# Differential attention on one core: the difference of the two maps moved from VectorE to GpSimd, the reciprocals moved ahead of the maxima

## The chip, the core and the metric

The kernel runs on one core of a Trainium2 chip. The metric is the device time of one execution in microseconds. Five engines run side by side, each with its own queue in order, and meet at semaphores: TensorE (PE; its weight loads are listed as PEld), VectorE (DVE), ScalarE (ACT), GpSimd (POOL) and SyncE (SP, which issues the DMAs).

## What is computed

The reference is one layer of a backbone, run for 128 context tokens and 1024 latent tokens: a SwiGLU feed-forward, then attention beside a recurrent unit, then a second feed-forward. The change touches the attention alone:

```python
# 4 heads; each has two maps (m = 0, 1) over 64 dimensions, values of 128
s = jnp.einsum('bqhmd,bkhmd->bhmqk', qi, k) * scale
p = jax.nn.softmax(s, axis=-1)
pd = p[:, :, 0] - lam * p[:, :, 1]
o = jnp.einsum('bhqk,bkhv->bqhv', pd, v)
...
o = _rmsnorm(o, subln_g) * (1.0 - lam_init)
mix = jnp.concatenate([o, rg], axis=-1) @ w_out
```

Context tokens attend to 128 keys, latent tokens to 1152 (1024 of their own and 128 cached).

## The kernel before

The attention stage is a pipeline over 36 tiles u = 0 to 35: 4 heads of 9 tiles with 128 queries each. The first tile of a head has the context queries and one group of 128 keys (a short tile), the other eight have nine groups (long tiles). Maps are not divided by their sums. With sums S0 and S1 of the exponentials, a tile keeps e0 + c * e1 with c = -lam * S0 / S1, and the attended values are multiplied by 1 / S0 at the end.

What a long tile needs, and on which engine:

- TensorE, `scores(u)` (L1011): two maps of 128 x 1152 into PSUM, in six pieces that alternate between the maps, `PIECES = ((0, 0, 512), (0, 512, 1024), (1, 0, 512), (0, 1024, UNIT), (1, 512, 1024), (1, 1024, UNIT))`. The first piece of map m waits for the exponential that read that map's banks before.
- VectorE, `maxima(u, m)` (L2221): the negated maximum of each row.
- ScalarE, `exps(u, m)` (L1540): the exponential into one of three buffers `pr`, with the row sums in `sums`; `e_done` counts them.
- VectorE, `difference(u)` (L2227, L2228, L2230): the reciprocals of the two sums, the coefficient `coef`, and one fused instruction that multiplies the second map by it and adds the first; `pd_ready` counts tiles.
- TensorE, `group(u, g)` (L1026): transposes of 3 x 3 blocks through one PSUM bank (bank 6). The first waits for `pd_ready`, each further one for the copy of the group before (`t_done`). ScalarE copies groups 0 and 2 (L1533), VectorE group 1 (`p_copy`, L2243).
- TensorE, `values(u, part)` (L1040), VectorE, `output(u)` (L2236): the values, and their scaling by 1 / S0. ScalarE squares them for the norm (L1548).

The order is written out by hand. In iteration u, TensorE does the scores of u, the transposes of u - 2 and the values of u - 3, mixed. VectorE does the maxima of u, the copy of u - 2, the difference of u - 1 and the output of u - 3. ScalarE does the copy of group 0 of u - 2, both exponentials of u, the copy of group 2, and the squares of u - 4. At iterations 35 and 36 VectorE also splits weights for the next stage (L1643), and from iteration 36 ScalarE and VectorE split the inputs of the output projection (L1564, L1567, L2250, L2253).

GpSimd does two things. It rotates the last head's keys (L672 to L675), which TensorE needs only at tile 27. And when VectorE has inverted the norms of the first three heads (L2274, iteration 32), it multiplies their outputs by them in 27 instructions of 128 x 128 (L682), chunk after chunk of 384 tokens. TensorE's `outputs(c, hd)` wait for these, at iteration 36 for chunk 0 and later for chunks 1 and 2.

Of the kernel before, what the change touches and what calls it, by code (L numbers as in the profile page):

```python
# [19 lines left out]
ALU = mybir.AluOpType  # L20
# [9 lines left out]
NC = T // CH  # L30
# [5 lines left out]
NH = 4  # L36
# [21 lines left out]
TILES = NH * QT  # L58
# [50 lines left out]
def build(nc, a, out):  # L109
    ctx = ExitStack()  # L110
    with ctx:
        def sem(name):
            return ctx.enter_context(nc.semaphore(name))

        def sb(name, shape, dt=F32, stack=ctx):
            return stack.enter_context(nc.sbuf_tensor("sb_" + name, shape, dt))
# [58 lines left out]
        with ExitStack() as s:  # L175
            cosT = sb("cosT", [P, LAT], F32, s)
            sinT = sb("sinT", [P, LAT], F32, s)
            swp = sb("swp", [P, LAT], F32, s)
# [5 lines left out]
            sums = sb("sums", [P, 3, 2], F32, s)  # L184
            rec = sb("rec", [P, 6, 2], F32, s)
            coef = sb("coef", [P, 3], F32, s)
            ss = sb("ss", [P, NH, 9], F32, s)
            lams = sb("lams", [P, 4], F32, s)
            nlam = sb("nlam", [P, 1], F32, s)
# [84 lines left out]
        lam_e = sem("lam_e")  # L274
        swapped = sem("swapped")
        roped = sem("roped")
        last_rope = sem("last_rope")
        s_ready = sem("s_ready")
        mx_ready = sem("mx_ready")
        e_done = sem("e_done")  # L280
        pd_ready = sem("pd_ready")
        t_ready = sem("t_ready")
        t_done = sem("t_done")
# [4 lines left out]
        o_rec = sem("o_rec")  # L288
        o_nrm_pool = sem("o_nrm_pool")
# [5 lines left out]
        w_ready = sem("w_ready")  # L295
        w_x = sem("w_x")
        y_done = sem("y_done")
        passed = [sem(f'passed{e}') for e in range(2)]
        y_out = sem("y_out")

        ssf = ss[:].rearrange("p h t -> p (h t)")
# [7 lines left out]
        def probs(u, m):  # L309
            return pr[:, u % 3, m, 0:KEY_TILES[u % QT] * P]  # L310
# [9 lines left out]
        def attended(hd, t):  # L320

            return o_first[:, t * P:(t + 1) * P] if hd == 0 else v[:, t, (hd - 1) * P:hd * P]

        def hv(h, c, k):

            return h[:, (c * KT + k) * CH:(c * KT + k + 1) * CH]
# [114 lines left out]
        def alone(eng):  # L441


            eng.sem_inc(passed[eng is nc.vector], 1)


        @blk.sync
# [218 lines left out]
        @blk.gpsimd  # L666
        def _(pool):

            xt = x[:, KT - 1, CTX:T]
            pool.wait_ge(acst, N_ACST)  # L670
            pool.wait_ge(swapped, 1)
            pool.tensor_tensor(xt, xt, cosT[:], ALU.mult).then_inc(last_rope, 1)  # L672
            pool.tensor_tensor(swp[:], swp[:], sinT[:], ALU.mult).then_inc(last_rope, 1)
            pool.wait_ge(last_rope, 2)
            pool.tensor_tensor(xt, xt, swp[:], ALU.add).then_inc(last_rope, 1)  # L675

            pool.wait_ge(o_rec, 1)
            for c in range(NC):
                for hd in range(NH - 1):
                    for t in range(3 * c, 3 * c + 3):  # L680
                        o = attended(hd, t)
                        m = pool.tensor_scalar(o, o, ss[:, hd, t:t + 1], None, ALU.mult)  # L682
                    m.then_inc(o_nrm_pool, 1)


        @blk.tensor
        def _(pe):

            def three(o, wH, wL, xH, xL, begin, end):

                pe.matmul(o, wH, xH, start=begin, stop=False)  # L691
                pe.matmul(o, wH, xL, start=False, stop=False)  # L692
                return pe.matmul(o, wL, xH, start=False, stop=end)  # L693
# [270 lines left out]
            for hf in range(2):  # L964
# [4 lines left out]
                for t in range(T // P):  # L969
# [4 lines left out]
                    for k in range(KT):  # L974
                        wv = slice((k % 4) * 256, (k % 4 + 1) * 256)
                        m = three(ps[:, n % 6, 0:256], hv(hH, t // 3, k)[:, tk], hv(hL, t // 3, k)[:, tk], wiH[:, k // 4, wv], wiL[:, k // 4, wv],
                                  k == 0, k == KT - 1)
# [38 lines left out]
            def group(u, g):  # L1016

                if 3 * g >= KEY_TILES[u % QT]:
                    return
                if g == 0:  # L1020
                    pe.wait_ge(pd_ready, u + 1)
                n = groups_before(u) + g
                if n:
                    pe.wait_ge(t_done, n)
                for k in range(3 * g, min(3 * g + 3, KEY_TILES[u % QT])):
                    m = pe.transpose(ps[:, 6, (k % 3) * P:(k % 3 + 1) * P], probs(u, 0)[:, k * P:(k + 1) * P], ident[:])  # L1026
                m.then_inc(t_ready, 1)
# [19 lines left out]
            for u in range(TILES + 3):  # L1047
                if u < TILES:
                    if u == (NH - 1) * QT:
                        pe.wait_ge(last_rope, 3)  # L1050
                    scores(u)
                for g in range(3):
                    if 0 <= u - 2 < TILES:
                        group(u - 2, g)
                    if g < 2 and 0 <= u - 3 < TILES:
                        values(u - 3, g)
                if u == TILES:
                    for hd in range(NH - 1):
                        outputs(0, hd)
# [571 lines left out]
        def _(dve):  # L1631
            chain = [0]

            def link(ins):

                chain[0] += 1
                ins.then_inc(step, 1)
                dve.wait_ge(step, chain[0])
# [456 lines left out]
            y, q, r = lnorm[:, 8:16], lnorm[:, 16:24], lnorm[:, 24:32]  # L2095
# [63 lines left out]
            for j in range(RGT):  # L2159
# [13 lines left out]
                for d in range(2):  # L2173
                    dve.wait_ge(rg_s, 2 * j + d + 1)
                    bx, r = x[:, 2 + 2 * d], x[:, 1 + 2 * d]
# [23 lines left out]
            for e in range(KT):  # L2199
# [3 lines left out]
                xt = x[:, e, CTX:T]  # L2203
# [16 lines left out]
                dve.wait_ge(s_ready, 2 * u + m + 1)  # L2220
                dve.tensor_reduce(nmx[:, u % 2, m:m + 1], unit(u, m), AX.X, ALU.max, negate=True).then_inc(mx_ready, 1)  # L2221

            def difference(u):

                r = u % 3
                dve.wait_ge(e_done, 2 * u + 2)
                link(dve.reciprocal(rec[:, u % 6], sums[:, r]))  # L2227
                link(dve.scalar_tensor_tensor(coef[:, r:r + 1], sums[:, r, 0:1], nlam[:, 0:1],  # L2228
                                              rec[:, u % 6, 1:2], ALU.mult, ALU.mult))
                dve.scalar_tensor_tensor(probs(u, 0), probs(u, 1), coef[:, r:r + 1], probs(u, 0), ALU.mult,  # L2230
                                         ALU.add).then_inc(pd_ready, 1)

            def output(u):

# [20 lines left out]

            dve.wait_ge(outs, 48)
            for u in range(TILES + 3):
                if u < TILES:
                    for m in range(2):
                        maxima(u, m)  # L2260
                p_copy(u - 2)
                if 1 <= u <= TILES:
                    difference(u - 1)
                if u >= 3:
                    output(u - 3)
                if u in (TILES - 1, TILES):
                    f = u - TILES + 1
                    lo(wiL[:, f], f, None, wiH[:, f], whi_wo + f + 1)
                if u == TILES + 1:
                    for k in MIX_ORDERS[0][:KT - 1]:  # L2270
                        mix_low(0, k)
                if u == (NH - 1) * QT + 5:
                    dve.wait_ge(o_sd, 1)
                    dve.reciprocal(ss[:, 0:NH - 1], ss[:, 0:NH - 1]).then_inc(o_rec, 1)  # L2274
# [158 lines left out]
```

## Time and profile before

| | us |
|---|---|
| median of 3 runs | 2306.4 |
| lowest and highest | 2306.05, 2315.53 |
| span of the profiled execution | 2307.2 |
| busy PE, DVE, ACT, POOL | 2221.6, 1541.2, 819.0, 27.1 |
| attention stage in the span | about 1173 to 1394 |

The profile is one execution. A page gives busy times, the chain of work that ended last and the costliest groups. The timeline gives instructions in order of time: start, duration, engine, line and operation, what is written and read, how many are merged in the row, and in brackets the idle time before and the engine whose work ended it. Where several instructions are merged, the duration is that of the whole row. Line numbers such as L2230 are those of the kernel before. Spans on POOL are rough; distances between starts are more solid.

### The profile page before, as it was taken

Reading aid. Unit: us, or ns where it says so; the run is one execution under the profiler, and the core shown is the slowest. Engines: PE = TensorE matmul, PEld = TensorE weight load, DVE = VectorE, ACT = ScalarE, POOL = GpSimd, SP = SyncE. Lnnn points to the kernel's source line nnn. Section 1 sums busy time; section 2 is a strip of 40 time slices with the busy share of each in tenths; the row PEclk is TensorE's granted clock in tenths of the full one; section 3 lists DMA queues with packets and bytes.
Section 4 is the critical chain, followed back from the end, with each engine's and each line's share of the span. In section 5 each row is a group of like instructions: output and inputs, shape, how many; then the busy total and the mean of one; then the engine's idle time right before and its main releaser. Section 6 shows DMA issues by size and latency. Waiting matters only on the chain.

```text
span 2307.2 us, 33872 instructions
## 1 busy us (share of the span) xinstructions
PE 2221.6 (96%) x13080; PEld 2117.2 (92%) x13080; DVE 1541.2 (67%) x2586; ACT 819.0 (35%) x1462; POOL 27.1 (1%) x34
## 2 busy tenths in 40 slices
PE   5989999999999999999989999999999999999997
PEld 3989999999999998778967779999999999999997
DVE  5977676777878775675558884586545456746556
ACT  5622222334111143654236663344323233412122
POOL 0000000000000000000010030000000000000000
PEclk9999999999999999999999999999999999999999
DMA  7433233244524303011000011222122223441212
GB/s 285 131 103 131 103 121 112 94 134 140 208 81 158 124 19 147 1 37 59 32 23 22 24 40 38 73 91 79 66 77 69 73 70 107 139 141 49 97 55 83
DMA packets 82288, 209.52 MB, mean 91 GB/s; under 512 B 9984, under 2 KB 36480, under 8 KB 82176
## 3 DMA queue, kind: packets, MB, share of 16 engines
q1 hardware_dynamic: 82176, 207.99, 26.6%
q8 instruction: 74, 1.21, 0.2%
q14 instruction: 38, 0.31, 0.0%
HBM read 172.04 MB, written 35.92 MB: 90 GB/s over the span
## 4 chain that ended last, share of the span: by engine, by line
PE 90%; DVE 6%; ACT 2%; issue 1%; DMA 1%; DVEq 0%; ACTq 0%
PE ps L691 18%; PE ps L693 17%; PE ps L692 17%; PE ps L783 9%; PE ps L784 9%; PE ps L785 9%; PE ps L1011 4%; PE ps L1040 2%; PE ps L950 2%; PE ps L1026 1%; DVE sb_nmx L2221 1%; PE ps L732 1%; DVE sb_hL L1719 1%; DVE sb_tmp L1728 1%; DVE sb_last_raw L1670 0%
## 5 line engine op out<-in xcount | busy, mean ns | idle before, releaser
L691 PE MATMUL ps<-sb_hH,sb_wH 128*128 128x384 f32 x1664 | 562.6, 338 | 6.3 <-DVE sb_hL L1719 2.9
L692 PE MATMUL ps<-sb_hL,sb_wH 128*128 128x384 f32 x1664 | 557.8, 335 | 0.0
L693 PE MATMUL ps<-sb_hH,sb_wL 128*128 128x384 f32 x1664 | 557.6, 335 | 0.0
L691 PEld LDWEIGHTS ps<-sb_hH,sb_wH 128*128 128x128 f32 x1664 | 313.7, 189 | 10.1 <-DVE sb_hL L1719 4.1
L692 PEld LDWEIGHTS ps<-sb_hL,sb_wH 128*128 128x128 f32 x1664 | 313.7, 188 | 1.1
L693 PEld LDWEIGHTS ps<-sb_hH,sb_wL 128*128 128x128 f32 x1664 | 313.6, 188 | 0.0
L2023 DVE SCALAR_TENSOR_TENSOR sb_x<-ps,sb_mod,sb_x 128x384 f32<-128x384 f32 (+2 forms) x384 | 186.4, 514 | 181.4 <-PE ps L693 176.6
L783 PE MATMUL ps<-sb_hH,sb_wH 128*128 128x384 f32 x704 | 235.4, 334 | 1.7 <-issue 0.9
L784 PE MATMUL ps<-sb_hL,sb_wH 128*128 128x384 f32 x704 | 235.2, 334 | 0.0
L785 PE MATMUL ps<-sb_hH,sb_wL 128*128 128x384 f32 x704 | 235.2, 334 | 0.0
L1330 ACT ACTIVATE sb_wH<-sb_raw 128x512 fp32r<-128x512 f32 (+1 forms) x96 | 57.0, 596 | 379.2 <-PE ps L693 371.2
L1196 ACT ACTIVATE sb_wH<-sb_wide 128x512 fp32r<-128x512 f32 x176 | 110.9, 633 | 225.9 <-DVE sb_wide L1773 220.7
L1185 ACT ACTIVATE sb_wH<-sb_raw 128x512 fp32r<-128x512 f32 x212 | 129.6, 626 | 171.4 <-PE ps L693 66.7
L783 PE MATMUL ps<-sb_r2H,sb_wH 128*128 128x384 f32 x528 | 177.1, 336 | 6.6 <-issue 6.6
L691 PE MATMUL ps<-sb_hH,sb_wiH 128*128 128x384 f32 x528 | 178.5, 338 | 3.4 <-DVE sb_wiL L1643 2.8
L1755 DVE TENSOR_TENSOR sb_wL<-sb_raw,sb_wH 128x512 fp32r<-128x512 f32 x212 | 139.9, 686 | 59.2 <-ACT sb_wH L1185 59.0
L784 PE MATMUL ps<-sb_r2L,sb_wH 128*128 128x384 f32 x528 | 176.9, 335 | 0.0
L785 PE MATMUL ps<-sb_r2H,sb_wL 128*128 128x384 f32 x528 | 176.9, 335 | 0.0
L693 PE MATMUL ps<-sb_hH,sb_wiL 128*128 128x384 f32 x528 | 176.6, 334 | 0.0
L692 PE MATMUL ps<-sb_hL,sb_wiH 128*128 128x384 f32 x528 | 176.5, 334 | 0.0
L783 PEld LDWEIGHTS ps<-sb_hH,sb_wH 128*128 128x128 f32 x704 | 132.2, 188 | 2.2 <-issue 2.2
L784 PEld LDWEIGHTS ps<-sb_hL,sb_wH 128*128 128x128 f32 x704 | 132.2, 188 | 0.0
(242 smaller groups left out, 3643.8 us busy)
## 6 DMA issues: line engine op xcount, KB each, us to landing
sb_raw<-in_w_gate SPq DMA_DIRECT2D x56, 512.0 KB, 3.5
sb_raw<-in_w_up SPq DMA_DIRECT2D x56, 512.0 KB, 3.5
sb_raw<-in_w_mod SPq DMA_DIRECT2D x56, 512.0 KB, 3.6
hidden<-sb_tmp SPq DMA_DIRECT2D x132, 192.0 KB, 2.3
sb_hid_raw<-hidden SPq DMA_DIRECT2D x40, 576.0 KB, 6.3
sb_raw<-in_w_dn SPq DMA_DIRECT2D x80, 256.0 KB, 2.7
sb_stage<-in_w_mod SPq DMA_DIRECT2D x4, 2048.0 KB, 15.0
sb_raw<-in_w_in SPq DMA_DIRECT2D x16, 512.0 KB, 3.8
```

The costliest lines, as they stand in the source:

```text
L691: pe.matmul(o, wH, xH, start=begin, stop=False)
L692: pe.matmul(o, wH, xL, start=False, stop=False)
L693: return pe.matmul(o, wL, xH, start=False, stop=end)
L783: pe.matmul(dst, wH[:, slot, at], opv(0, b, k), start=begin and k == 0, stop=False, skip_group_check=True)
L784: pe.matmul(dst, wH[:, slot, at], opv(1, b, k), start=False, stop=False, skip_group_check=True)
L785: m = pe.matmul(dst, wL[:, slot, at], opv(0, b, k), start=False, stop=k == 3, skip_group_check=True)
L1011: mm = pe.matmul(unit(u, m)[:, b:e], x[r, hd, q * P:(q + 1) * P], keys, start=True, stop=True, tile_position=(m * DH, 0))
L1185: act.activation(wH[:, o if slot is None else slot], raw_of(o, other), ACT.Copy).then_inc(one_hi[o], 1)
L1196: act.activation(wH[:, at], wide[:, 8 + at], ACT.Copy).then_inc(sum_hi, 1)
L1330: act.activation(wH[:, down_slot(t), 0:w], raw[:, s // 2, s % 2 * 512:s % 2 * 512 + w], ACT.Copy).then_inc(dn_hi, 1)
L1755: dve.tensor_tensor(wL[:, at], raw_of(o, other), wH[:, at].bitcast(F32), ALU.subtract).then_inc(one_lo[o], 1)
L2023: m = dve.scalar_tensor_tensor(x[:, t, b:e], ps[:, DOWN_BANKS[n % 6], b - c * CH:e - c * CH], mod[:, gate + t, cond:cond + 1], x[:, t, b:e ...
```

## The change

GpSimd makes the difference in three dependent instructions per tile: the coefficient, the second map times the coefficient, and the sum. VectorE keeps the reciprocals, now at the beginning of an iteration, ahead of the maxima; a new semaphore `rec_ready` hands them over. The norms of chunk 0 are spread on GpSimd between the differences of tiles 32 to 35; the rest follow the last difference. Two counting semaphores elsewhere become one (`passed`), which nothing waits for.

```diff
+            def difference(u):
+                r = u % 3
+                pool.wait_ge(rec_ready, u + 1)
+                pool.tensor_scalar(coef[:, r:r + 1], sums[:, r, 0:1], nlam[:, 0:1], rec[:, u % 6, 1:2], ALU.mult,
+                                   ALU.mult).then_inc(pool_step, 1)
+                pool.wait_ge(pool_step, 3 + 2 * u + 1)
+                pool.tensor_scalar(probs(u, 1), probs(u, 1), coef[:, r:r + 1], None, ALU.mult).then_inc(pool_step, 1)
+                pool.wait_ge(pool_step, 3 + 2 * u + 2)
+                pool.tensor_tensor(probs(u, 0), probs(u, 0), probs(u, 1), ALU.add).then_inc(pd_ready, 1)
+
+            def output_norm(c, hd):
+                for t in range(3 * c, 3 * c + 3):
+                    o = attended(hd, t)
+                    m = pool.tensor_scalar(o, o, ss[:, hd, t:t + 1], None, ALU.mult)
+                m.then_inc(o_nrm_pool, 1)
+
+            first = TILES - NH
+            for u in range(TILES):
+                difference(u)
+                if u == first:
+                    pool.wait_ge(o_rec, 1)
+                if first <= u < first + NH - 1:
+                    output_norm(0, u - first)
+            for c in range(1, NC):
                 for hd in range(NH - 1):
-                    for t in range(3 * c, 3 * c + 3):
-                        o = attended(hd, t)
-                        m = pool.tensor_scalar(o, o, ss[:, hd, t:t + 1], None, ALU.mult)
-                    m.then_inc(o_nrm_pool, 1)
+                    output_norm(c, hd)
...
-            def difference(u):
-
-                r = u % 3
+            def reciprocals(u):
+
                 dve.wait_ge(e_done, 2 * u + 2)
-                link(dve.reciprocal(rec[:, u % 6], sums[:, r]))
-                link(dve.scalar_tensor_tensor(coef[:, r:r + 1], sums[:, r, 0:1], nlam[:, 0:1],
-                                              rec[:, u % 6, 1:2], ALU.mult, ALU.mult))
-                dve.scalar_tensor_tensor(probs(u, 0), probs(u, 1), coef[:, r:r + 1], probs(u, 0), ALU.mult,
-                                         ALU.add).then_inc(pd_ready, 1)
+                dve.reciprocal(rec[:, u % 6], sums[:, u % 3]).then_inc(rec_ready, 1)
...
             for u in range(TILES + 3):
+                if 1 <= u <= TILES:
+                    reciprocals(u - 1)
                 if u < TILES:
                     for m in range(2):
                         maxima(u, m)
                 p_copy(u - 2)
-                if 1 <= u <= TILES:
-                    difference(u - 1)
                 if u >= 3:
                     output(u - 3)
```

## Rows read from the trace of the kernel before

**Rows 1.** The page: busy time by engine, then the chain that ended last.
```profile
PE 2221.6 (96%) x13080; PEld 2117.2 (92%) x13080; DVE 1541.2 (67%) x2586; ACT 819.0 (35%) x1462; POOL 27.1 (1%) x34
...
PE 90%; DVE 6%; ACT 2%; issue 1%; DMA 1%; DVEq 0%; ACTq 0%
```
**Rows 2.** Timeline, two long tiles (start, duration, engine, line; idle before in brackets).
```profile
1203.00 2.37 PE L1011 MATMUL ps<-sb_x 64*128 64x512 f32 x8
1203.13 0.21 ACT L1540 ACTIVATION_READ_ACCUMULATOR sb_pr<-ps,sb_nmx 128x1 f32 x1
...
1205.24 2.62 DVE L2221 TENSOR_REDUCE sb_nmx<-ps 128x1 f32<-128x1152 f32 x2 [0.75 <-PE ps L1011]
...
1205.53 0.55 PE L1026 MATMUL ps<-sb_ident,sb_pr 128*128 128x128 f32 x3
...
1207.78 0.55 DVE L2243 COPY sb_pT<-ps 128x384 f32<-128x384 f32 x1
...
1208.38 0.31 PEld L1026 LDWEIGHTS ps<-sb_ident,sb_pr 128*128 128x128 f32 x3 [0.16 <-DVE sb_pT L2243]
...
1208.43 0.22 DVE L2228 SCALAR_TENSOR_TENSOR sb_coef<-sb_sums,sb_nlam,sb_rec 128x1 f32<-128x1 f32 x1
1208.69 1.42 DVE L2230 SCALAR_TENSOR_TENSOR sb_pr<-sb_pr,sb_coef 128x1152 f32<-128x1152 f32 x1
...
1211.39 0.55 PE L1026 MATMUL ps<-sb_ident,sb_pr 128*128 128x128 f32 x3
```
**Rows 3.** Groups by line and shape, 1180 to 1400 us: busy, mean, idle before.
```profile
L1026 PE MATMUL ps<-sb_ident,sb_pr 128*128 128x128 f32 x292 | 51.7, 285 | 9.0 <-DVE sb_pT L2243 3.4 <-ACT sb_pT L1533 2.8 <-DVE sb_pr L2230 2.8
```
**Rows 4.** Timeline, end of the first head; last row: the same place of the second.
```profile
1219.62 1.22 ACT L1540 ACTIVATE sb_pr<-ps,sb_nmx 128x1152 f32<-128x1152 f32 x1
...
1225.47 1.22 ACT L1540 ACTIVATE sb_pr<-ps,sb_nmx 128x1152 f32<-128x1152 f32 x1
...
1226.44 0.89 PE L1011 MATMUL ps<-sb_x 64*128 64x128 f32 x4
...
1227.74 0.55 PE L1026 MATMUL ps<-sb_ident,sb_pr 128*128 128x128 f32 x3 [0.42 <-DVE sb_pr L2230]
...
1233.17 0.55 PE L1026 MATMUL ps<-sb_ident,sb_pr 128*128 128x128 f32 x3
...
1278.72 0.55 PE L1026 MATMUL ps<-sb_ident,sb_pr 128*128 128x128 f32 x3 [0.42 <-DVE sb_pr L2230]
```
**Rows 5.** Timeline, the last tiles of the stage.
```profile
1362.06 1.21 ACT L1540 ACTIVATE sb_pr<-ps,sb_nmx 128x1152 f32<-128x1152 f32 x1
...
1368.05 0.16 DVE L2227 RECIPROCAL sb_rec<-sb_sums 128x2 f32<-128x2 f32 x1
...
1368.69 1.43 DVE L2230 SCALAR_TENSOR_TENSOR sb_pr<-sb_pr,sb_coef 128x1152 f32<-128x1152 f32 x1
...
1380.23 1.52 DVE L2230 SCALAR_TENSOR_TENSOR sb_pr<-sb_pr,sb_coef 128x1152 f32<-128x1152 f32 x1
...
1381.81 0.55 PE L1026 MATMUL ps<-sb_ident,sb_pr 128*128 128x128 f32 x3 [1.33 <-DVE sb_pr L2230]
1381.94 1.21 DVE L1643 TENSOR_TENSOR sb_wiL<-sb_raw,sb_wiH 128x1024 fp32r<-128x1024 f32 x1
...
1386.27 0.55 PE L1026 MATMUL ps<-sb_ident,sb_pr 128*128 128x128 f32 x3 [0.23 <-DVE sb_pr L2230]
...
1388.82 0.50 ACT L1533 ACTIVATE sb_pT<-ps 128x384 f32<-128x384 f32 x1
1389.37 0.55 PE L1026 MATMUL ps<-sb_ident,sb_pr 128*128 128x128 f32 x3 [1.39 <-ACT sb_pT L1533]
```
**Rows 6.** Timeline of POOL alone: the rotation and the norms.
```profile
1176.33 2.34 POOL L673 TENSOR_TENSOR sb_swp<-sb_swp,sb_sinT 128x1024 f32<-128x1024 f32 x1
1178.74 2.34 POOL L675 TENSOR_TENSOR sb_x<-sb_x,sb_swp 128x1024 f32<-128x1024 f32 x1
1363.64 1.76 POOL L682 TENSOR_SCALAR sb_raw<-sb_raw,sb_ss 128x128 f32<-128x128 f32 x3 [182.56 <-DVE sb_ss L2274]
1365.38 3.50 POOL L682 TENSOR_SCALAR sb_v<-sb_v,sb_ss 128x128 f32<-128x128 f32 x6
1368.85 2.88 POOL L682 TENSOR_SCALAR sb_raw<-sb_raw,sb_ss 128x128 f32<-128x128 f32 x3
...
1378.05 5.56 POOL L682 TENSOR_SCALAR sb_v<-sb_v,sb_ss 128x128 f32<-128x128 f32 x6
```

More of the change, by code:

```diff
@@ L276, in build @@
         roped = sem("roped")
-        last_rope = sem("last_rope")
+        pool_step = sem("pool_step")
         s_ready = sem("s_ready")
@@ L280, in build @@
         e_done = sem("e_done")
+        rec_ready = sem("rec_ready")
         pd_ready = sem("pd_ready")
@@ L297, in build @@
         y_done = sem("y_done")
-        passed = [sem(f'passed{e}') for e in range(2)]
+        passed = sem("passed")
         y_out = sem("y_out")
@@ L441, in alone @@
         def alone(eng):
-            eng.sem_inc(passed[eng is nc.vector], 1)
+            eng.sem_inc(passed, 1)
         @blk.sync
@@ L671, in _ @@
             pool.wait_ge(swapped, 1)
[L672 to L678, printed above, removed]
+            pool.tensor_tensor(xt, xt, cosT[:], ALU.mult).then_inc(pool_step, 1)
+            pool.tensor_tensor(swp[:], swp[:], sinT[:], ALU.mult).then_inc(pool_step, 1)
+            pool.wait_ge(pool_step, 2)
+            pool.tensor_tensor(xt, xt, swp[:], ALU.add).then_inc(pool_step, 1)
+            def difference(u):
[20 more added lines that the diff above has]
+            for c in range(1, NC):
                 for hd in range(NH - 1):
-                    for t in range(3 * c, 3 * c + 3):
-                        o = attended(hd, t)
-                        m = pool.tensor_scalar(o, o, ss[:, hd, t:t + 1], None, ALU.mult)
-                    m.then_inc(o_nrm_pool, 1)
+                    output_norm(c, hd)
         @blk.tensor
@@ L1049, in _ @@
                     if u == (NH - 1) * QT:
-                        pe.wait_ge(last_rope, 3)
+                        pe.wait_ge(pool_step, 3)
                     scores(u)
```

## The prediction

> **What bounds the kernel now.** I read the profile from the outside in. The page's first and fourth parts come first [rows 1]: TensorE is busy 96% of the span and carries 90% of the chain that ended last, VectorE 6%, and GpSimd (POOL) does almost nothing. The change touches only the attention stage, from about 1173 to 1394 us, some 220 us of 2307. So even a tenth of that stage is only 1% of the time.
>
> Next comes the timeline of two tiles in the middle of a head [rows 2]. A long tile takes 5.86 us (scores start at 1203.00; the same transposes come at 1205.53 and, one tile later, at 1211.39). I followed the loop that sets this. The first maximum starts at 1205.24, as soon as its scores are there, after VectorE has sat idle 0.75 us for them. Two maxima take 2.62 us and end at 1207.86; the copy of the middle third of the transposed map (L2243) ends at 1208.33; the transposes that waited 0.16 for it start at 1208.38 and take about 0.5; the next tile's scores need 2.24 from their start to the point where the maximum can begin (1203.00 to 1205.24). 1208.38 + 0.5 + 2.24 = 1211.1, which is 1205.24 + 5.86: the loop closes without slack. The difference (L2230, 1.42 us) and the two small instructions ahead of it are not in this loop: they run between the copy and the next maxima, where VectorE would otherwise wait. The change takes them away and leaves the loop as it is.
>
> Where does the difference end a wait? The grouped rows say it at once [rows 3]: TensorE's transposes L1026 sat idle 9.0 us in the whole stage, and only 2.8 of these end with L2230. The timelines place the 2.8: 0.42 us at the end of each of three heads (two of them in [rows 4]), 1.33 us ahead of tile 34 and 0.23 ahead of tile 35 [rows 5]. So the most that a free difference could return is 3 x 0.42 + 1.33 + 0.23 = 2.8 us, 0.12%.
>
> **The change part by part.** (a) *VectorE loses* 36 coefficients (0.22 us) and 36 differences (1.42, short 0.35). In the loop of [rows 2] this only makes the idle time ahead of the maxima longer, from 0.75 to about 2.5 us: worth 0. What is late next is the same thing as before, the scores.
>
> (b) *The reciprocals go ahead of the maxima.* They now wait there for the second exponential of the tile before, and the maxima, the copy and the output are queued behind that wait. In [rows 2] the accumulator of that exponential is read by 1203.34, 1.9 us before the maximum can start. Moreover the scores of the first map end only after pieces of the second, which wait for the same exponential. The reciprocal (0.15 us) is covered by what VectorE idles: 0. If the cover went, it would be 36 x 0.15 = 5 us.
>
> (c) *GpSimd gains three dependent instructions for each tile*, with a wait on its own semaphore between them. None of the wide ones is in the trace, so I bound them by the nearest rows [rows 6]. For the narrow ones I take distances between starts, since the page calls POOL's spans rough. The sum of two maps: 1024 columns with two inputs take 2.34 us, so 1152 take 2.34 x 1.125 = 2.6. The product by a column: 128 columns with one input take 3.50 / 6 = 0.58 us, and how this grows with width is the open point of this case. Low end: the width above 128 costs half of the two-input price of 2.34 / 1024 = 2.3 ns a column, which gives 0.58 + 1024 x 1.15 ns = 1.75 us. Middle: the full two-input price, 0.58 + 2.3 = 2.9. High end: everything in the 0.58 is width, 9 x 0.58 = 5.2. The coefficient, one column with two scalars, is at most about one narrow product: 0.5. Three handovers cost 0.3 together (end of L673 to start of L675 is 0.07, VectorE to POOL and the coefficient's own step I put at as much or a little more). I call the sum T: 0.5 + 1.75 + 2.6 + 0.3 = 5.2 us at the low end, 6.3 in the middle, 8.6 at the high end. I take 5.2, because one stream to read instead of two is the plain difference of the two instructions, and because most of a 0.58 us instruction of 128 columns must be fixed cost if 128 columns of two inputs cost only 0.29 us of width.
>
> The Trainium skill speaks of this price. "GPSIMD Engine Reference", section 4.1, calls one-input work there roughly line-rate, and section 3.1 gives a clock of 1.2 GHz; by an estimate from these the product takes about 0.58 + 0.85 = 1.4 us and T 4.8 to 4.9. The same page says in its key points that VectorE is about twice as fast for elementwise work, which speaks against the change; the sum of 2.6 us against 1.42 for the whole fused difference agrees.
>
> (d) *Does T fit?* A tile's difference may start when the second exponential is done (1203.34, plus the reciprocal: about 1203.6) and is first read by the transposes at 1211.39: 7.8 us for T, at one every 5.86. At T = 5.2 nobody waits in the middle of a head. At a head's end the room is less [rows 4]: tile 7's second exponential ends at 1219.62 + 1.22 + 0.2 for its accumulator = 1221.0, and TensorE, whose scores for the short tile take 0.89, comes at 1227.3 instead of 1227.74. That is 6.1 us. For tile 8 it is 1226.9 to 1233.17 - 0.42, again less the reciprocal: 5.7 us. Both hold 5.2, so each of three head ends gives back its 0.42: **-1.3 us**.
>
> (e) *The last tiles.* The norms of the first outputs (nine, 1.75 us for three) now stand between the differences of tiles 32 to 35 on GpSimd's queue, where they had an idle engine before. Tile 32's exponential is done at 1363.4 [rows 5]. From there GpSimd is back to back: T + 1.75 for each tile, against 5.86 of the loop. Difference 34 ends at 1363.5 + 3T + 3.5 = 1382.6 (before: 1381.75) and difference 35 at 1363.5 + 4T + 5.25 = 1389.6 (before: 1386.22). Of these 3.3 us some are covered: the transposes of tile 35 were followed by a wait for ScalarE, which came to its copy only at 1388.82, and the second three started at 1389.37. With the difference at 1389.6, the first three and the values behind them take 1.55, and the second three start at 1391.15: **+1.8 us**.
>
> (f) *A port.* The same rows show that the two engines hold each other up. Three norms took 2.88 us instead of 1.76 while L2230 ran (the rows of POOL and of L2230 at 1368.69), and the last six norms took 5.56 instead of 3.50 beside L2230 and L1643 [rows 5, 6]. L2230 is gone, but the two L1643 (1.21 us each, two inputs from SBUF) still run, now beside the differences of tiles 34 and 35. One of them can push difference 35: I take **+1.2**, between 0 and 2.4. The maxima and the copies read PSUM. Reciprocals at 0.15 to 0.16 beside busy POOL were not longer. The skill's "SBUF — State Buffer", section "Who interferes with whom", describes it as an exclusive lock against a VectorE instruction with two SBUF inputs; by it nothing in the loop contends, and the sum stays.
>
> The norms of the later chunks (18, 10.5 to 14 us) now start at about 1390 instead of 1368.85 and end by 1404. The first six are done by 1394 and are asked for after 1401; they are hidden. Should they hold up the low parts of the mix on VectorE, there are some 2 us of cover.
>
> Sum: -1.3 + 1.8 + 1.2 = +1.7 on the profiled execution, whose span of 2307.2 lies 0.8 above the median of 2306.4. Forecast: 2306.4 + 1.7, about **2308 us**, no change that can be measured.
>
> **The rivals.** *R1, GpSimd becomes the bound (slower).* A head takes 1278.72 - 1227.74 = 50.98 us [rows 4], in which GpSimd has eight long differences and a short one of about 1.8. Its queue is full from 8T + 1.8 = 51, T = 6.15. Above that every head costs 8(T - 6.15), and the end 4(T - 4.75). At T = 6.3 this is 5 + 6 and the port's 1.2, about +12: 2318. At T = 8.6 it is 4 x 20 + 15: about 2400. For it: the 0.58 us of a narrow product, for which no wide one is known. Against: two inputs at 2.3 ns a column would have to be no dearer than one.
>
> *R2, the difference was free to take away (a little faster).* T at 4.8 or less and no push by the port: the three 0.42 come back and most of the 1.56 at the end is eaten by the norms: -1.3 to -2.8, 2303.6 to 2305. It is the same mechanism as the forecast with the other end of two prices.
>
> *R3, the change does not reach VectorE's gain because the reciprocal waits.* If the second exponential came late, or the lock held the reciprocal, the maxima would be late by up to 1 us in 32 tiles: +10 to +30. The 1.9 us of room in [rows 2] speak against it.
>
> *R4, faster by over 0.5%.* It would need 0.36 us less a tile, and TensorE itself idles only 0.16 us in 5.86. I see no place for it.
>
> **How the numbers follow.** Forecast and its surroundings, T from 5.0 to 6.15: 0.5 (2305 to 2315). R2: 0.2. R1: 0.24, of which a fifth would still lie within 0.5% of before. R3: 0.04. R4: 0.02. About 0.5% (11.5 us) is what a measurement of this kernel can tell from no change. Slower by over 0.5%: 0.24. Same: 0.74. Faster: 0.02. The range starts at the largest gain, 2306.4 - 2.8 = 2303.6, and ends at 2322, where the product's price is just above that of a two-input one (T about 6.4); beyond it lie some 0.18.
>
> **What would show it.** A wide POOL product of 1.5 to 2.0 us and a sum of 2.6; tiles still 5.86 us apart; VectorE's idle time before L2221 up to about 2.5 us; no wait of L1026 for POOL inside a head; transposes of tile 35 later by about 2 us than the shift of the rest. The prediction is wrong if the product takes 2.9 us or more, or if L1026 waits for POOL in every tile.

## The result and the profile after

The changed kernel is slower: 2332.6 us against 2310.2 us of before on the same chip (medians of 4 runs each), ratio 1.0089, interval 1.0063 to 1.0114. The profiled execution has a span of 2325.3 us against 2307.2, +18.1. The prediction was 2308 with a range up to 2322; it was wrong. Of the 24.6 us between 2308 and 2332.6, 3.8 lie in the base: the prediction started from 2306.4, the median of three runs of before, and with the fourth it is 2310.2.

The page of after: busy time, then the chain that ended last, by engine and by line.

```profile
PE 2224.8 (96%) x13080; PEld 2121.1 (91%) x13080; DVE 1496.3 (64%) x2514; ACT 817.0 (35%) x1462; POOL 227.4 (10%) x142
...
PE 82%; POOL 8%; DVE 5%; ACT 2%; issue 1%; DMA 1%; SPq 0%; DVEq 0%; ACTq 0%
PE ps L713 17%; PE ps L714 17%; PE ps L715 17%; PE ps L805 9%; PE ps L806 9%; PE ps L807 9%; POOL sb_pr L685 4%; POOL sb_pr L687 3%; PE ps L972 2%; PE ps L754 1%; DVE sb_hL L1741 1%; PE ps L1033 1%; DVE sb_tmp L1750 1%; ACT sb_pr L1562 1%; DVE sb_last_raw L1692 0%
```

GpSimd, which in [rows 1] was on no part of the chain, now holds 8% of it. 8% of 2325 is 186 us, most of the attention stage's 238. That VectorE is busy 45 us less is not worth anything by itself. Groups by line and shape, 1170 to 1420 us (mean in ns; idle before; releasers): the product is L685, the sum L687, the coefficient L682, the transposes L1048 (L1026 before).

```profile
L685 POOL TENSOR_SCALAR sb_pr<-sb_pr,sb_coef 128x1152 f32<-128x1152 f32 x32 | 102.3, 3198 | 3.0
...
L687 POOL TENSOR_TENSOR sb_pr<-sb_pr 128x1152 f32<-128x1152 f32 x32 | 84.3, 2636 | 2.7
...
L682 POOL TENSOR_SCALAR sb_coef<-sb_sums,sb_nlam,sb_rec 128x1 f32<-128x1 f32 x36 | 12.0, 334 | 9.5 <-DVE sb_rec L2248 9.5
...
L1048 PE MATMUL ps<-sb_ident,sb_pr 128*128 128x128 f32 x292 | 52.5, 288 | 24.0 <-POOL sb_pr L687 19.7 <-DVE sb_pT L2260 2.6 <-ACT sb_pT L1555 1.6
```

The product took 3.20 us, where the prediction took 1.75. The sum (2.64) and the coefficient (0.33) are as foreseen. TensorE now waits 19.7 us for GpSimd ahead of its transposes, where it waited 2.8 for the difference on VectorE [rows 3]. The timeline of the first head's end shows how the waits arise.

```profile
1217.58 0.34 POOL L682 TENSOR_SCALAR sb_coef<-sb_sums,sb_nlam,sb_rec 128x1 f32<-128x1 f32 x1
...
1221.59 0.17 DVE L2248 RECIPROCAL sb_rec<-sb_sums 128x2 f32<-128x2 f32 x1 [0.43 <-ACT sb_pr L1562]
...
1223.90 0.34 POOL L682 TENSOR_SCALAR sb_coef<-sb_sums,sb_nlam,sb_rec 128x1 f32<-128x1 f32 x1
...
1224.33 3.20 POOL L685 TENSOR_SCALAR sb_pr<-sb_pr,sb_coef 128x1152 f32<-128x1152 f32 x1
...
1227.11 0.88 PE L1033 MATMUL ps<-sb_x 64*128 64x128 f32 x4
...
1227.61 2.61 POOL L687 TENSOR_TENSOR sb_pr<-sb_pr 128x1152 f32<-128x1152 f32 x1
...
1230.28 0.55 PE L1048 MATMUL ps<-sb_ident,sb_pr 128*128 128x128 f32 x3 [2.29 <-POOL sb_pr L687]
...
1236.59 0.55 PE L1048 MATMUL ps<-sb_ident,sb_pr 128*128 128x128 f32 x3 [0.86 <-POOL sb_pr L687]
...
1240.38 0.34 POOL L682 TENSOR_SCALAR sb_coef<-sb_sums,sb_nlam,sb_rec 128x1 f32<-128x1 f32 x1 [2.29 <-DVE sb_rec L2248]
```

From coefficient to coefficient it is 6.32 us, GpSimd's time T for a tile, against 5.86 for the loop of [rows 2]. Tile 7's reciprocals were ready at 1221.76 and GpSimd took them up at 1223.90: a backlog of 2.1 us. It was 0.1 at tile 3 and grew by about 0.5 (6.32 - 5.86) with each tile. Inside the first head the room of 7.8 us hides it. At the short tile TensorE comes early and waits 2.29, then 0.86 for tile 8. Then GpSimd itself waits 2.29, since the next head's first long tile is not ready. In the second and the third head the backlog reaches 2.6 us, and transposes inside the head wait too, 0.31, 0.59 and 0.58 us at tiles 13 to 15:

```profile
1272.03 0.55 PE L1048 MATMUL ps<-sb_ident,sb_pr 128*128 128x128 f32 x3 [0.59 <-POOL sb_pr L687]
```

To compare runs I use marks: the starts of the scores of the short tiles 9, 18 and 27 (the row of 1227.11 above; 1226.44 in [rows 4]) and the first matmul of the output projection, 1393.75 before and 1411.76 after.

| stretch, us | before | after |
|---|---|---|
| stage's first scores to tile 9 | 53.67 | 53.66 |
| tile 9 to 18 | 50.97 | 54.37 |
| tile 18 to 27 | 50.99 | 54.37 |
| tile 27 to the projection | 65.35 | 75.91 |
| sum | 220.98 | 238.31 |

17.3 of the 18.1 us lie in three stretches: 3.4 for each of two heads and 10.6 in the last one, which holds the third head's end and the end of the stage. There another thing is added. Timeline of the last differences in after:

```profile
1380.70 1.76 POOL L693 TENSOR_SCALAR sb_raw<-sb_raw,sb_ss 128x128 f32<-128x128 f32 x3
...
1393.63 1.33 DVE L1665 TENSOR_TENSOR sb_wiL<-sb_raw,sb_wiH 128x1024 fp32r<-128x1024 f32 x1
...
1394.20 3.22 POOL L687 TENSOR_TENSOR sb_pr<-sb_pr 128x1152 f32<-128x1152 f32 x1
...
1397.48 0.90 PE L1048 MATMUL ps<-sb_ident,sb_pr 128*128 128x128 f32 x3 [3.83 <-POOL sb_pr L687]
...
1398.17 2.34 PE L1062 MATMUL ps<-sb_v,sb_pT 128*128 128x128 f32 x10
...
1403.05 3.52 DVE L1665 TENSOR_TENSOR sb_wiL<-sb_raw,sb_wiH 128x1024 fp32r<-128x1024 f32 x1
...
1405.54 0.55 PE L1048 MATMUL ps<-sb_ident,sb_pr 128*128 128x128 f32 x3 [1.49 <-POOL sb_pr L687]
```

The norms (1.76 for three) stand in GpSimd's queue; the sum beside the weights' split L1665 takes 3.22 instead of 2.62, and the second split 3.5 instead of 1.21. TensorE waits 3.83 and 1.49 us (and 1.93 one tile earlier, at 1388.82). Ten value matmuls then take 2.34 us, where the same ten take 1.28 elsewhere. The stretches of the span say why (granted clock third from the right), first the end of the stage in before, then in after:

```profile
1375.00:1385.00 10.00, 8.67 (x67) 7.25 (x66) 8.47 (x14) 4.80 (x12) 8.62 (x10) 1.00 0.44 129
1385.00:1395.00 10.00, 7.80 (x62) 7.12 (x61) 7.23 (x13) 5.46 (x17) 0.00 (x0) 1.00 0.28 97
```
```profile
1385.00:1395.00 10.00, 6.72 (x38) 5.41 (x35) 4.81 (x6) 3.98 (x11) 9.74 (x8) 0.83 0.32 120
1395.00:1405.00 10.00, 6.57 (x36) 6.33 (x36) 2.81 (x4) 2.38 (x7) 9.82 (x7) 0.66 0.15 53
```

After the waits for GpSimd, TensorE was granted its lower level (1.2 GHz) for part of the time.

### The profile page after: what moved, and what is told of

Read it like the earlier page. It is cut to its first block, busy times and chain, and to the rows that moved or that the text cites. A ratio compares the mean times of both kernels' runs of the same rounds, so it can differ in the third digit from the quotient of the medians.

```text
span 2325.3 us, 33908 instructions
## 1 busy us (share of the span) xinstructions
PE 2224.8 (96%) x13080; PEld 2121.1 (91%) x13080; DVE 1496.3 (64%) x2514; ACT 817.0 (35%) x1462; POOL 227.4 (10%) x142
## 3 DMA queue, kind: packets, MB, share of 16 engines
q8 instruction: 74, 1.21, 0.2%
## 4 chain that ended last, share of the span: by engine, by line
PE 82%; POOL 8%; DVE 5%; ACT 2%; issue 1%; DMA 1%; SPq 0%; DVEq 0%; ACTq 0%
PE ps L713 17%; PE ps L714 17%; PE ps L715 17%; PE ps L805 9%; PE ps L806 9%; PE ps L807 9%; POOL sb_pr L685 4%; POOL sb_pr L687 3%; PE ps L972 2%; PE ps L754 1%; DVE sb_hL L1741 1%; PE ps L1033 1%; DVE sb_tmp L1750 1%; ACT sb_pr L1562 1%; DVE sb_last_raw L1692 0%
```

## The experiments

Theory A: the loss is GpSimd's time per tile, T = 6.32 us, and in it the product's price. Rivals: the place of the reciprocals; handovers and the port that the two engines share; the norms in the queue. Stretches are those of the table (tile 9 to 18, 18 to 27, 27 to the projection); ratios are against before on the same chip. TensorE's clock ahead of tile 9 differs from run to run: the stage's first scores, which stand ahead of all that is changed, start between 1172.2 and 1178.3 us, and those of tile 9 up to 8 us later than before's 1226.44. The spans of the profiled executions carry this, so they are less exact than these stretches.

| run | T, us | 9 to 18 | 18 to 27 | last | ratio (interval) |
|---|---|---|---|---|---|
| before | | 50.97 | 50.99 | 65.35 | |
| after | 6.32 | 54.37 | 54.37 | 75.91 | 1.0089 (1.0063, 1.0114) |
| reciprocals ahead only | | 51.18 | 51.19 | 65.16 | 1.0008 (0.9997, 1.0019) |
| no product | 3.1 | 50.47 | 50.48 | 64.25 | 0.9996 (0.9985, 1.0006) |
| product over 704 | 5.2 | 50.47 | 50.47 | 68.24 | 1.0006 (0.9992, 1.0021) |
| product over 1024 | 5.97 | 51.02 | 51.56 | 71.52 | 1.0034 (1.0020, 1.0048) |
| norms on VectorE | 6.32 | 54.38 | 54.39 | 72.96 | 1.0054 (1.0037, 1.0071) |
| product as two-input | 5.25 | 50.47 | 50.47 | 71.38 | 1.0010 (0.9997, 1.0023) |
| both of these | 5.25 | 50.48 | 50.47 | 65.10 | 0.9999 (0.9986, 1.0013) |
| split by columns | | 50.81 | 50.80 | 66.52 | 1.0006 (0.9990, 1.0021) |
| late reciprocals | 6.32 | 88.91 | 84.80 | 111.69 | 1.0609 (1.0585, 1.0633) |
| product twice | 9.6 | 81.98 | 79.35 | 111.41 | 1.0551 (1.0529, 1.0573) |

**Reciprocals ahead only** (before, with this alone):

```diff
+            def reciprocals(u):
+                dve.wait_ge(e_done, 2 * u + 2)
+                link(dve.reciprocal(rec[:, u % 6], sums[:, u % 3]))
...
+                if 1 <= u <= TILES:
+                    reciprocals(u - 1)
                 if u < TILES:
                     for m in range(2):
                         maxima(u, m)
```

> Only the reciprocals are moved ahead of the maxima; coefficient and difference stay on VectorE where they were. Theory A (GpSimd's time per tile, 6.32 us against the loop's 5.86, makes the loss): span as before, 2307 within 1 us, tiles 5.86 us apart, VectorE's idle time ahead of the maxima 0.6 instead of 0.75. Rival B (the wait for the second exponential ahead of the maxima makes the loss): tiles further apart, 0.2 to 0.5 us each, span 2313 or more.

The two heads grew by 0.2 us each, the last stretch shrank by 0.2, and the ratio is no change. Span 2316.6, not the 2307 expected: 7.8 of the 9.4 us lie ahead of tile 9, where TensorE had the lower clock for longer. The rival is out at 0.2 us a head.

**No product**:

```diff
                 pool.tensor_scalar(coef[:, r:r + 1], sums[:, r, 0:1], nlam[:, 0:1], rec[:, u % 6, 1:2], ALU.mult,
-                                   ALU.mult).then_inc(pool_step, 1)
-                pool.wait_ge(pool_step, 3 + 2 * u + 1)
-                pool.tensor_scalar(probs(u, 1), probs(u, 1), coef[:, r:r + 1], None, ALU.mult).then_inc(pool_step, 1)
+                                   ALU.mult).then_inc(pool_step, 2)
```

> The kernel after without GpSimd's product: the second map is added without its coefficient (that part of the computation is left out); coefficient, sum and handovers stay, T about 3.1 us. Theory A: GpSimd is off the path everywhere; the three waits of 0.42 at the heads' ends and those of the last tiles (1.33, 0.23) are gone: 1.3 to 2.8 us below before, span 2304.5 to 2306. Rivals (handover latency, or the two engines holding each other up, make the loss): at least half of the 18 us stays, span 2316 or more.

Heads at 50.47, 0.5 below before; last stretch 1.1 below: 2.1 us in all over the three stretches, as the free difference should give. Everything that was lost hangs on the product's time. In the ratio 2 us cannot be told from nothing. The span was 2313.3, not the 2304.5 to 2306 expected; 7.3 us of it lie ahead of tile 9.

**Product over 704 columns**, the T of the prediction:

```diff
-                pool.tensor_scalar(probs(u, 1), probs(u, 1), coef[:, r:r + 1], None, ALU.mult).then_inc(pool_step, 1)
+                w = min(704, KEY_TILES[u % QT] * P)
+                pool.tensor_scalar(probs(u, 1)[:, 0:w], probs(u, 1)[:, 0:w], coef[:, r:r + 1], None, ALU.mult).then_inc(pool_step, 1)
```

> The kernel after with the product over only the first 704 of 1152 columns (the rest of the second map is added without its coefficient). At the measured 3.20 us for 1152 and 0.60 for 128 the product takes about 2.06 and T 5.2 us, the value of the prediction. Theory A, and the prediction's own sum if the price was its only fault: -1.3 at the heads, +1.8 and +1.2 at the end, +1.7 in all, span 2309 (2307 to 2311). If the sum itself is wrong (a threshold lower than 6.15), 5 us or more above before.

The heads give back 0.5 each; the last stretch costs 2.9: +1.9 us for the three stretches, against the +1.7 of the prediction (span 2311.6, of which 2.6 ahead of tile 9). Its end (timeline):

```profile
1381.12 2.62 POOL L688 TENSOR_TENSOR sb_pr<-sb_pr 128x1152 f32<-128x1152 f32 x1
1381.32 3.50 DVE L1666 TENSOR_TENSOR sb_wiL<-sb_raw,sb_wiH 128x1024 fp32r<-128x1024 f32 x1
...
1383.71 2.74 POOL L694 TENSOR_SCALAR sb_v<-sb_v,sb_ss 128x128 f32<-128x128 f32 x3
...
1383.79 0.89 PE L1049 MATMUL ps<-sb_ident,sb_pr 128*128 128x128 f32 x3 [2.27 <-POOL sb_pr L688]
...
1389.00 3.30 POOL L688 TENSOR_TENSOR sb_pr<-sb_pr 128x1152 f32<-128x1152 f32 x1
```

The port is seen both ways: the split started 0.2 us behind the sum and took 3.50 instead of 1.21; the norms behind it 2.74 instead of 1.76; the last sum 3.30 instead of 2.62. That is 1.7 us on GpSimd's queue, where I had put 1.2.

**Product over 1024 columns** (the same edit with 1024), to tell two laws of the head apart:

> The kernel after with the product over 1024 of 1152 columns (the rest of the second map is added without its coefficient), T = 6.315 - 128 x 2.57 ns = 5.99 us. It tells two laws of the heads apart, read in the distance between the short tiles' scores (50.47 us when GpSimd is never late, 54.37 in after). Law of the prediction's rival (queue full over the whole head, from T = 6.15): 50.5. New law (between a short tile and the next head's first reciprocal GpSimd must idle 2.3 us, so the head takes 8T + 3.9 with 1.6 for the short difference, from T = 5.82): 51.8.

51.56 in the settled head (51.02 in the one before), against 51.8 and 50.5: the new law. With the measured T of 5.965 it gives 8 x 5.965 + 3.9 = 51.6. GpSimd's idle time is in its own timeline:

```profile
1290.21 0.33 POOL L682 TENSOR_SCALAR sb_coef<-sb_sums,sb_nlam,sb_rec 128x1 f32<-128x1 f32 x1
1290.63 0.60 POOL L686 TENSOR_SCALAR sb_pr<-sb_pr,sb_coef 128x128 f32<-128x128 f32 x1
1291.32 0.46 POOL L688 TENSOR_TENSOR sb_pr<-sb_pr 128x128 f32<-128x128 f32 x1
1294.06 0.33 POOL L682 TENSOR_SCALAR sb_coef<-sb_sums,sb_nlam,sb_rec 128x1 f32<-128x1 f32 x1 [2.28 <-DVE sb_rec L2249]
```

A head on GpSimd is eight long differences, a short one of 1.6 and an idle 2.3. What it waits for is seen in after. Tile 8's difference ends at 1236.53 and its transposes start at 1236.59. ScalarE copies their result first and makes tile 10's exponentials behind it, and VectorE's reciprocals of tile 10 follow:

```profile
1237.17 0.49 ACT L1555 ACTIVATE sb_pT<-ps 128x384 f32<-128x384 f32 x1 [2.87 <-PE ps L1048]
1237.56 1.22 ACT L1562 ACTIVATE sb_pr<-ps,sb_nmx 128x1152 f32<-128x1152 f32 x1
...
1238.76 1.22 ACT L1562 ACTIVATE sb_pr<-ps,sb_nmx 128x1152 f32<-128x1152 f32 x1
...
1240.10 0.17 DVE L2248 RECIPROCAL sb_rec<-sb_sums 128x2 f32<-128x2 f32 x1 [0.24 <-ACT sb_pr L1562]
```

From 1236.53 to the next coefficient at 1240.38 it is 3.85 us, in which GpSimd has only the short difference to do.

**Norms of chunk 0 on VectorE**:

```diff
-                if u == first:
-                    pool.wait_ge(o_rec, 1)
-                if first <= u < first + NH - 1:
-                    output_norm(0, u - first)
...
+                if 0 <= u - (NH - 1) * QT - 5 < NH - 1:
+                    hd = u - (NH - 1) * QT - 5
+                    for t in range(3):
+                        o = attended(hd, t)
+                        m = dve.tensor_scalar(o, o, ss[:, hd, t:t + 1], None, ALU.mult)
+                    m.then_inc(o_nrm_pool, 1)
```

> The kernel after with the nine norms of chunk 0 on VectorE, in its idle time, instead of between GpSimd's last differences. Theory A: the heads still cost about 9 us, the end loses 5.25 us of queue and so 4 to 5 of its 8: span 2320 to 2321. Rival C (the norms in the queue make most of the loss): span 2312 or less. If GpSimd does not bind the last tiles: 2325, no change.

Heads as in after, last stretch 3.0 less in the profile (expected 4 to 5). The ratio moved by 0.35%, 8 us, with intervals of 0.2% and 0.25% on either side. So the norms are a part of the end and none of the heads; the profile puts the part at 3 us, the ratio at 8 with some 7 us of uncertainty either way. The span was 2321.7, just above the 2320 to 2321 expected; rival C is out.

**Product as a two-input instruction**:

```diff
-                pool.tensor_scalar(probs(u, 1), probs(u, 1), coef[:, r:r + 1], None, ALU.mult).then_inc(pool_step, 1)
+                pool.tensor_tensor(probs(u, 1), probs(u, 1), coef[:, r:r + 1].to_broadcast([P, KEY_TILES[u % QT] * P]), ALU.mult).then_inc(pool_step, 1)
```

> The kernel after with GpSimd's product written as a two-input instruction whose second input is the coefficient, repeated over the columns. If the width of a two-input instruction costs 2.62 us for 1152 columns whatever the second input is, T is 5.7 to 5.8, below 5.86. Theory A: heads at most 0 to 1 us each, end +3 to +5: span 2309 to 2314. Rivals (handover latency or contention): like after, 2325.

Group of that run:

```profile
L685 POOL TENSOR_TENSOR sb_pr<-sb_pr,sb_coef 128x1152 f32<-128x1152 f32 x32 | 67.4, 2106 | 2.7
```

2.11 us for the same product, a third less than 3.20, and less than I expected. The heads' loss is gone, the result is the same. The span was 2317.0, 4.8 of it ahead of tile 9, where 2309 to 2314 was expected. The last stretch still costs 6.0, more than the 3 to 5 expected. That is 3.1 more than with 704 columns at nearly the same T. TensorE's waits for GpSimd are nearly the same in the two runs (2.39 and 2.95 us here, 2.27 and 2.74 there), but its granted clock was 0.86 and 0.67 in the two stretches from 1380 to 1400, against 0.83 and 1.00. Why it stayed at the lower level for longer here is open.

**Both** (two-input product, norms on VectorE):

> The product as a two-input instruction with the repeated coefficient (T 5.25) and the norms of chunk 0 on VectorE. If price and queue at the end are the whole cause: heads 50.47 as in the run with the two-input product, last stretch 65.35 of before less up to 1.1, plus 0 to 1.5 for the weights' split that meets GpSimd: stage 216 to 219 against 218.6, a ratio of 0.999 to 1.000. If moving the difference has another price at the end, the last stretch stays at 68 or more.

50.48, 50.47 and 65.10: 1.3 us below before in the stretches, nothing measurable in the ratio. All 17.3 us of the loss are given back by one cheaper form and nine moved instructions, with the difference still on GpSimd. Here the nine norms were worth 6.3 us of the last stretch (71.38 to 65.10), where with the dear product they were worth 3.0.

**Split by columns**: VectorE makes coefficient and the first 768 columns, GpSimd the last 384 (its side of the edit is shown).

```diff
+                r, n, w = u % 3, u // QT * (QT - 1) + u % QT - 1, slice(6 * P, 9 * P)
+                pool.wait_ge(rec_ready, u + 1)
+                pool.tensor_scalar(probs(u, 1)[:, w], probs(u, 1)[:, w], coef[:, r:r + 1], None, ALU.mult).then_inc(pool_step, 1)
+                pool.wait_ge(pool_step, 3 + 2 * n + 1)
+                pool.tensor_tensor(probs(u, 0)[:, w], probs(u, 0)[:, w], probs(u, 1)[:, w], ALU.add).then_inc(pool_step, 1)
```

> Reciprocals and coefficient on VectorE ahead of the maxima; VectorE makes the difference of the first 768 columns where it always did, GpSimd product and sum of the last 384 (about 1.25 + 0.87 us). TensorE waits for GpSimd only ahead of its third group. VectorE's part takes 1.0 instead of 1.42: the 0.42 at the heads' ends go, 0.8 to 1.2 of the 1.56 at the end too: 2 to 2.4 us below before, ratio 0.999. If the two engines hold each other up (VectorE's fused difference reads two SBUF inputs), VectorE's part takes up to 2 us now and then and it is as before or 1 to 3 us slower.

Heads 0.2 below before, last stretch 1.2 above: no change, and not the 2 us hoped for. The fused difference over 768 columns took 1.01 us and was never held up. Part of the last stretch is TensorE's clock, which was 0.50 in the last 5 us: the last values took 3.78 us, where the same 16 matmuls take 2.05 in before.

```profile
1395.82 3.78 PE L1063 MATMUL ps<-sb_v,sb_pT 128*128 128x128 f32 x16 [0.58 <-ACT sb_pT L1556]
```

**Late reciprocals** (after, with them behind the copy again):

```diff
-                if 1 <= u <= TILES:
-                    reciprocals(u - 1)
                 if u < TILES:
                     for m in range(2):
                         maxima(u, m)
                 p_copy(u - 2)
+                if 1 <= u <= TILES:
+                    reciprocals(u - 1)
```

> The kernel after with the reciprocals back behind the copy, where the difference was. They are then done about 4.7 us later in a tile, 3.0 us before the next tile's transposes ask for the difference, and these set the copy and with it the next reciprocals. Theory A with this loop: T + group 0 and values + copy = about 6.3 + 2.3 + 0.6 = 9.2 us a tile, +3.3 over 32 tiles, span about 2410. If the place of the reciprocals matters little: 2325 to 2330.

+6.1%. The loop is there, and it is longer than expected, 10.6 us a tile instead of 9.2. Timeline:

```profile
1237.58 0.34 POOL L682 TENSOR_SCALAR sb_coef<-sb_sums,sb_nlam,sb_rec 128x1 f32<-128x1 f32 x1 [2.83 <-DVE sb_rec L2248]
...
1243.95 0.90 PE L1048 MATMUL ps<-sb_ident,sb_pr 128*128 128x128 f32 x3 [3.41 <-POOL sb_pr L687]
...
1244.64 2.34 PE L1062 MATMUL ps<-sb_v,sb_pT 128*128 128x128 f32 x10
...
1247.92 0.15 DVE L2248 RECIPROCAL sb_rec<-sb_sums 128x2 f32<-128x2 f32 x1
...
1248.18 0.34 POOL L682 TENSOR_SCALAR sb_coef<-sb_sums,sb_nlam,sb_rec 128x1 f32<-128x1 f32 x1 [4.29 <-DVE sb_rec L2248]
```

The values in the loop take 2.34 instead of 1.28 us: the granted clock was 0.77 of full from 1240 to 1300 us. So at T = 6.32 the move of the reciprocals ahead of the maxima is a needed part of the change: without it the loss is 6.1% instead of 0.9%.

**Product twice**:

> The kernel after with the product made twice (the second map is then scaled by the square of its coefficient): T 6.32 + 3.27 = 9.6 us. Theory A: GpSimd's queue never empties, 32 long tiles cost 3.27 us more each, less what it idled (about 2.3 us a head): span 2325 + 105 - 9 = about 2420. Rivals: a doubling of 3.2 us that shows less than 60 us in the span.

The marks moved by 21, 28, 25 and 35 us against after, 109 in all where about 95 were expected. 32 x 3.29 is 105, and the four short tiles add 0.7 us each. The expectation took off 9 us of idle time that did not go: at the three heads' ends GpSimd still idled 2.89, 2.89 and 1.58 us. But for these waits its queue is full, and every microsecond on it shows. TensorE's granted clock was 0.83 of full from 1200 to 1300 us.

**Instructions of GpSimd by themselves**, on its idle time in the kernel before, four of a kind (two with two full inputs), each waiting for the one ahead:

```diff
+            for w in (1, 128, 256, 512, 1024):
+                sw, one = swp[:, 0:w], cosT[:, 0:1]
+                for n in range(4):
+                    probe(pool.tensor_scalar(sw, sw, one, None, ALU.mult))
+                for n in range(4):
+                    probe(pool.tensor_scalar(sw, sw, 1.0, None, ALU.mult))
+                for n in range(4):
+                    probe(pool.tensor_tensor(sw, sw, one.to_broadcast([P, w]), ALU.mult))
+                for n in range(2):
+                    probe(pool.tensor_tensor(sw, sw, cosT[:, 0:w], ALU.mult))
```

> The kernel before, with extra instructions on the idle GpSimd in the attention stage, in series: products over 1, 128, 256, 512 and 1024 columns with the scalar in SBUF, with a constant, as two-input instructions with a repeated column, and with two full inputs. From after: 0.33 us at one column, 0.60 at 128, 3.20 at 1152, so 0.27 + 2.54 ns a column; if it is a line, 0.93 at 256, 1.58 at 512, 2.88 at 1024. A constant scalar should save a part of the fixed 0.27 only. Two full inputs at 1024: 2.34. The span should stay near before, a little longer where the difference on VectorE and these instructions meet.

Groups (scalar in SBUF, constant, repeated column, two full inputs; then three of them at 128 columns):

```profile
L688 POOL TENSOR_SCALAR sb_swp<-sb_swp,sb_cosT 128x1024 f32<-128x1024 f32 x4 | 11.4, 2842 | 0.4
...
L690 POOL TENSOR_SCALAR sb_swp<-sb_swp 128x1024 f32<-128x1024 f32 x4 | 11.1, 2768 | 0.3
...
L692 POOL TENSOR_TENSOR sb_swp<-sb_swp,sb_cosT 128x1024 f32<-128x1024 f32 x4 | 8.6, 2141 | 0.3
...
L694 POOL TENSOR_TENSOR sb_swp<-sb_swp,sb_cosT 128x1024 f32<-128x1024 f32 x2 | 4.7, 2353 | 0.2
...
L688 POOL TENSOR_SCALAR sb_swp<-sb_swp,sb_cosT 128x128 f32<-128x128 f32 x4 | 2.4, 609 | 0.4
...
L692 POOL TENSOR_TENSOR sb_swp<-sb_swp,sb_cosT 128x128 f32<-128x128 f32 x4 | 1.6, 398 | 0.3
...
L694 POOL TENSOR_TENSOR sb_swp<-sb_swp,sb_cosT 128x128 f32<-128x128 f32 x2 | 0.9, 454 | 0.2
```

Some of these means contain a wait of one instruction of the four beside VectorE's difference, which shows in the row of least, middle and greatest duration (ns):

```profile
L692 POOL TENSOR_TENSOR sb_swp<-sb_swp,sb_cosT x4: 1892/1892/2887, 1255.0 to 1261.0; 128x1024 f32<-128x1024 f32 x4
```

By the least durations, the product with a scalar takes 0.60, 0.92, 1.56 and 2.84 us at 128, 256, 512 and 1024 columns, which is the line expected. The two-input one takes 0.40, 0.61, 1.04 and 1.89 with the repeated column and 0.45, 0.73, 1.27 and 2.35 with two full inputs. So the instruction with one stream is the dearer one, at every width. A constant instead of the scalar saves 0.07. The instructions themselves made the stage 8 us longer than before's (226.99 against 218.56 from the first maximum to the projection; one execution), of which 6 in the head in which the wide ones ran. VectorE's difference had a mean of 2.12 instead of 1.42 there and its coefficient 0.49 instead of 0.22:

```profile
L2249 DVE SCALAR_TENSOR_TENSOR sb_pr<-sb_pr,sb_coef 128x1152 f32<-128x1152 f32 x9 | 19.1, 2120 | 0.3
```

## Why the prediction was wrong

**What bounds the kernel, (a) and (b)**: right. The loop of [rows 2] did not move; with GpSimd never late a head takes 50.47, and the first stretches are the same to 0.01. The most that a free difference could give was put at 2.8 us; without the product the stretches gave 2.1. Reciprocals ahead cost 0.2 us a head alone, where I had put 0. VectorE's idle time ahead of the maxima came to 1.7 us, with 0.4 more ahead of the reciprocals, where 2.5 was foreseen.

**(c), the price of the product**: this is the step that failed. I had its bounds from both sides, 1.75, 2.9 and 5.2 us, and took the low one, arguing that one stream costs less than two and that the 0.58 us of a narrow product is mostly fixed. Measured: 3.20, that is 0.27 + 2.54 ns a column, above the middle bound, and past the 2.9 that the prediction had named as the sign of being wrong. T came to 6.32, not 5.2. The row that I called nearest, the two-input instruction of [rows 6], taken at its full price gave 2.9, near the measured time; halving it rested on no row. The Trainium skill ("GPSIMD Engine Reference", section 4.1) calls one-input work roughly line-rate; by the estimate in the prediction that gives 1.4 us. The trace contradicts it for this instruction by more than a factor of two. The page's rate did not enter the sum, yet it leans the same way as my choice, and I gave the rival that contradicts it only 0.24.

**The sum itself** held at its own T. The run with T = 5.2 gave +1.9 for a forecast of +1.7: -1.0 at two heads and +2.9 in the last stretch, against -0.84 for two heads and, with the third, +2.6. That it fits to 0.3 us is in part luck: the port took 1.7 where I had put 1.2, and in the stretch from 1380 to 1390 the granted clock was 0.83, for which the sum has no term.

**(d), the threshold**: the rival R1 named the mechanism and, at T = 6.3, +12 us; it was +17.3. Its law let GpSimd work through the whole head, from T = 6.15. But after the short tile GpSimd idles 2.3 us, because the next head's reciprocals hang on the transposes that have just waited. A head takes 8T + 3.9, and the loss begins at (50.47 - 3.9) / 8 = 5.82. For T = 6.32 that is 54.4, as measured; my law gave a loss of 1.4 a head where it was 3.4. The waits inside the second and third head, which the prediction's signs excluded, belong to it. With the measured T, R1's own terms give 5.4 + 6.3 + 1.2 = +13, or 2319, still inside the range; so the price alone does not carry the time out of the range. The rest is this law, the clock below and the 3.8 us of the base.

**(e) and (f), the end**: my formula for the last difference, its start plus 4T + 5.25, gives 1374.39 + 25.3 + 5.25 = 1404.9 in after's trace; the sum ended at 1405.5, the 0.6 being the port (3.22 instead of 2.62). Both terms were right for a given T. What I had not priced is TensorE's lower clock after the waits, 0.83 and 0.66 of full in two stretches of 10 us. The Trainium skill's exclusive lock ("SBUF — State Buffer", section "Who interferes with whom") agrees with the 3.50 us of a split that takes 1.21 alone.

**R3 and R4**: neither came. **What stays open**: the medians differ by 22 us, the ratio says 21 (15 to 26), and the profiled executions differ by 18. The profile places 17.3 us in three stretches of the stage; whether the rest is the clock at the stage's two ends, which differs from run to run, was not settled. Nor was how the 10.6 us of the last stretch divide between GpSimd's queue and TensorE's clock.

## What to carry to other kernels

Before work is moved to another engine, take its price at the real width, or take the bound that a row supports and not a fraction of it; where the margin is 0.5 us in 6, that one number decides. Compare an engine's time per tile not with the loop's time alone but with each place where the pipeline drains: there backlog comes due and the engine then idles. And try another form of the same operation: here a third of the product's time lay in the choice between a scalar operand and a repeated column.

## What the runs showed of the hardware

- GpSimd, float32 in SBUF: multiplying 1152 columns by a per-partition scalar takes 3.20 us, the same as a two-input instruction with a repeated column 2.11, a two-input sum 2.61 to 2.63 where nothing held it up. A constant in place of the scalar changes little (2.77 against 2.84 at 1024).
- GpSimd's sum and VectorE's two-input instruction hold each other up in both directions: 1.21 us became 3.50, 2.62 became 3.30. Beside GpSimd's wide products VectorE's fused difference had a mean of 2.12 instead of 1.42.
- VectorE's reciprocal of two columns was never held up by a busy GpSimd: it took 0.15 to 0.17 us in every run.
- At the end of after's stage TensorE waited 1.93, 3.83 and 1.49 us for GpSimd; the granted clock was 0.83 and 0.66 of full in the two stretches of 10 us, and ten matmuls behind the first two waits took 2.34 instead of 1.28 us. The waits of 2.29 and 0.86 at the first head's end left the same ten at 1.28. With the reciprocals late or the product made twice, where TensorE waited in nearly every tile, the clock was 0.81 and 0.82 from 1180 to 1520 us.
